# Probabilities times V with V as the stationary operand, two heads side by side on two column groups

## The reference, cut to what matters

```
branch A: logits over the top-k admissible keys, probs = softmax(logits)
          attn_a = probs @ v
branch B: window of 128 plus the own chunk, one learned sink per head in the denominator
          attn_b = (p @ v) / denom
o_a = (attn_a * silu(z_a)) @ w_oa        o_b = (attn_b * silu(z_b)) @ w_ob
y   = x + gate * ((sigmoid(g_a) * o_a + sigmoid(g_b) * o_b) @ w_out)
```

## Time and profile before

| what | us |
|---|---|
| median of 3 runs (1081.9 to 1086.25) | 1082.78 |
| the profiled execution, its own time | 1083.33 |
| its span | 1081.5 |
| PE busy / weight loads busy | 1035.2 / 920.8 |
| DVE / ACT / POOL busy | 676.3 / 408.9 / 323.3 |
| L1613, matmuls by V, forms with `VA`: 576 instructions, busy | 74.9 |

### The profile page before, as it was taken

How to read it: one execution, slowest core, us unless ns; L and a number is a source line. 1 busy time by engine, 2 the same in 40 slices (tenths; PEclk the granted TensorE clock), 3 DMA queues, 4 the chain that set the end, 5 groups by cost and what they waited for, 6 DMA issues and landing times.

```text
span 1081.5 us, 18078 instructions
## 1 busy us (share of the span) xinstructions
PE 1035.2 (96%) x6569; PEld 920.8 (85%) x6569; DVE 676.3 (63%) x1437; ACT 408.9 (38%) x1239; POOL 323.3 (30%) x348
## 2 busy tenths in 40 slices
PE   6976999999999999999999999999999999999998
PEld 1336888787799999999998998888888689999998
DVE  2647337699999999999951676555464454331111
ACT  0245456544432322222113676665564452212000
POOL 0034003221243532122124434332130034536432
PEclk9988999999999999999999799999999979999999
DMA  9822001473332323232134732112100646524332
GB/s 348 329 74 64 23 32 64 121 243 101 98 95 81 108 79 116 78 90 88 48 134 152 253 100 72 35 60 74 35 23 20 191 150 196 163 82 132 122 121 75
DMA packets 100586, 120.83 MB, mean 112 GB/s; under 512 B 11128, under 2 KB 83592, under 8 KB 99352
## 3 DMA queue, kind: packets, MB, share of 16 engines
q1 hardware_dynamic: 95344, 114.48, 33.5%
q10 hardware_dynamic: 5160, 5.24, 1.4%
HBM read 89.72 MB, written 35.95 MB: 116 GB/s over the span
## 4 chain that ended last, share of the span: by engine, by line
PE 85%; issue 4%; DVE 3%; ACT 3%; DMA 2%; POOL 2%; SPq 0%; POOLq 0%; DVEq 0%
PE PS L1360 18%; PE PS L1362 18%; PE PS L1361 18%; PE PS L1613 9%; PE PS L1589 6%; PE PS L1534 4%; PE PS L1369 4%; PE PS L1553 2%; PE PS L1592 2%; PE PS L1435 2%; POOL YO L872 1%; DVE HL L1155 1%; DVE XT L1173 1%; PE PS L1539 1%; DMA WADA<-in_w_ada 1%
## 5 line engine op out<-in xcount | busy, mean ns | idle before, releaser
L1362 PE MATMUL PS<-HH,WL 128*128 128x384 f32 (+1 forms) x576 | 187.9, 326 | 0.0
L1360 PE MATMUL PS<-HH,WH 128*128 128x384 f32 (+1 forms) x576 | 187.8, 326 | 0.0
L1361 PE MATMUL PS<-HL,WH 128*128 128x384 f32 (+1 forms) x576 | 187.7, 326 | 0.0
L1214 DVE MAX8 M<-SC 128x8 f32<-128x384 f32 (+3 forms) x210 | 174.8, 870 | 10.5 <-DVE SC L1219 10.0
L1219 DVE MATCH_REPLACE8 SC<-M,SC 128x384 f32<-128x384 f32 (+3 forms) x210 | 180.0, 864 | 0.0
L767 POOL TENSOR_TENSOR WL<-RAW,WH 128x512 fp32r<-128x512 f32 (+1 forms) x80 | 100.6, 1263 | 246.4 <-ACT WH L888 246.4
L1360 PE MATMUL PS<-WH,HH 128*128 128x512 f32 (+3 forms) x288 | 110.3, 383 | 8.1 <-DVE HL L1155 7.9
L1361 PE MATMUL PS<-WL,HH 128*128 128x512 f32 (+3 forms) x288 | 108.7, 377 | 0.0
L1362 PE MATMUL PS<-WH,HL 128*128 128x512 f32 (+3 forms) x288 | 108.5, 377 | 0.0
L1360 PEld LDWEIGHTS PS<-HH,WH 128*128 128x128 f32 x576 | 108.1, 188 | 0.1
L1361 PEld LDWEIGHTS PS<-HL,WH 128*128 128x128 f32 x576 | 108.1, 188 | 0.0
(11 more groups left out here) (180 smaller groups left out, 2066.1 us busy)
## 6 DMA issues: line engine op xcount, KB each, us to landing
RAW<-in_w_all SPq DMA_DIRECT2D x72, 256.0 KB, 2.7
WADA<-in_w_ada SPq DMA_DIRECT2D x8, 1536.0 KB, 20.3
gz<-STG SPq DMA_DIRECT2D x48, 192.0 KB, 1.8
snat<-STG SPq DMA_DIRECT2D x24, 256.0 KB, 2.0
QKV<-snat SPq DMA_DIRECT2D x8, 768.0 KB, 6.0
GT<-gz SPq DMA_DIRECT2D x32, 192.0 KB, 2.5
XN<-in_x_prompt SPq DMA_DIRECT2D x8, 512.0 KB, 16.9
btad<-bvd ACTq DMA_DIRECT2D x4, 1024.0 KB
```

The lines of the kernel that those rows point to most:

```text
L1214: V.max(M8[0:r, a, :], w).then_inc(sel_step, 1)
L1360: T.matmul(out, wh, mh, start=first, stop=False)
L1361: T.matmul(out, wh, ml, start=False, stop=False)
L1362: return T.matmul(out, wl, mh, start=False, stop=last)
```

## The change

1. PE takes the units in pairs. Heads are reordered to 0, 4, 1, 5, 2, 6, 3, 7, so that a pair has one head of each key/value head. In even steps s PE multiplies units s - 4 and s - 3; for every block of keys and both heads in turn, V (128 keys x 64) is the stationary operand and `PT` (128 keys x 128 queries) the moving one. The output is transposed already, 64 x 128, and goes to partitions 0 to 63 for the first head and 64 to 127 for the second.
2. The "A" transposes, `ATTN` and the multiplication into it are gone. The reciprocals are taken in step 8g + 9, written to device memory in transposed order (`rdd`), and read back broadcast over 64 partitions per key/value head (`RB`, two transfers, step 8g + 10). SP loads z straight to `ATS`, POOL multiplies it by `RB` in step 8g + 15, DVE multiplies bank 6 + branch by that in step 8g + 16, SP writes it out in step 8g + 17. For the last group the three are at 8g + 11, 12 and 13.
3. `PT` has three buffers in place of two. `PT2`, `XNB`, `XG`, `LG1` and `RB` lie at other addresses, `RDEN` has two buffers, the slots of `GT` are used in another order, and the columns of z and the rows of `w_oa` and `w_ob` are permuted on the host to match the order of the pairs.

```
         VBS = at("VBS", [128, 2, 128], F32, 132608)
-        XNB = at("XNB", [128, 20, HD], F32, XB + 6144)
-        XG = at("XG", [128, 20, HD], F32, XB + 12288)
-        LG = [at("LG0", [128, 1024], F32, XB), at("LG1", [128, 1024], F32, XB + 17408)]
-        ATTN = [at("ATTN0", [128, 512], F32, XB + 4096), at("ATTN1", [128, 512], F32, 67584)]
+        XNB = at("XNB", [128, 20, HD], F32, XB + 8192)
+        XG = at("XG", [128, 20, HD], F32, XB + 13312)
+        LG = [at("LG0", [128, 1024], F32, XB), at("LG1", [128, 1024], F32, XB + 4096)]
...
-        ZT = at("ZT", [128, 4, 128], F32, XB + 21504)
-        PT = at("PT", [128, 2, 1024], F32, SCB + 8192)
+        RB = at("RB", [128, 4, 128], F32, 67584)
+        PT = [at("PT0", [128, 1024], F32, SCB + 8192), at("PT1", [128, 1024], F32, SCB + 12288),
+              at("PT2", [128, 1024], F32, XB + 18432)]
...
 
-        UNITS = [(tt, br, h) for tt in range(NT) for br in range(2) for h in range(8)]
+        HEADS = [4 * (i % 2) + i // 2 for i in range(8)]
+        UNITS = [(tt, br, h) for tt in range(NT) for br in range(2) for h in HEADS]
         NU = len(UNITS)
...
             TP[16 * (2 + i) + 6].append(("C", i, 0))
-        for g in range(2 * NT):
-            TP[8 * g + 15].append(("A", g // 2, g % 2))
         TQ = [(s, x) for s in range(S0, S1) for x in TP[s]]
...
         LOAD_AT, NORM_AT, SPLIT_AT = -7, -5, 2
+        NG2 = 2 * NT
+        ZR_AT = {8 * g + (15 if g < NG2 - 1 else 11): g for g in range(NG2)}
+        FIN_AT = {8 * g + (16 if g < NG2 - 1 else 12): g for g in range(NG2)}
+        OUT_AT = {8 * g + (17 if g < NG2 - 1 else 13): g for g in range(NG2)}
 
...
         for q, (_, x) in enumerate(TQ):
-            if x[0] == "A":
-                EV.append("V")
-            elif x[0] == "P" and unit_keys(x[1]) > 512:
+            if x[0] == "P" and unit_keys(x[1]) > 512:
                 EV.append("SV"[x[2]])
...
                 full, part = min(4, nk // 128), nk % 128 if nk < 512 else 0
-                dst = PT[:, u % 2, 512 * j:512 * (j + 1)].rearrange("p (b n) -> p b n", b=4)
-                if u >= 2:
-                    eng.wait_ge(pv_pe, u - 1)
+                dst = PT[u % 3][:, 512 * j:512 * (j + 1)].rearrange("p (b n) -> p b n", b=4)
+                if u >= 3:
+                    eng.wait_ge(pv_pe, (u - 3) // 2 + 1)
                 if full:
...
                 last = copy(QT[x[1] % 2][:, 4 * x[2]:4 * x[2] + 4, 0:r], src[:, :, 0:r])
-            elif x[0] == "A":
-                g, r = 2 * x[1] + x[2], rows_of(x[1])
-                if g >= 2:
-                    eng.wait_ge(att_out[g % 2], 16 * (g // 2))
-                eng.wait_ge(zt_in, 16 * (g + 1))
-                last = nc.vector.tensor_tensor(ATS[:, g % 2, :, 0:r], src[:, :, 0:r], ZT[:, :, 0:r], ALU.mult)
             else:
...
                     sp.dma_start(QKV[0:rows_of(tt), tt % 2, :], snat[tcols(tt), :]).then_inc(qkv_in[tt % 2], 16)
-                if s % 8 == 0 and 8 <= s < NU + 8:
+                if s % 8 == 1 and 9 <= s < NU + 8:
                     g = s // 8 - 1
+                    r = rows_of(g // 2)
+                    if g >= 2:
+                        sp.wait_ge(att_out[g % 2], 16 * (g // 2))
+                    sp.dma_start(ATS[:, g % 2, :, 0:r],
+                                 gz[512 * (g % 2):512 * (g % 2) + 512, tcols(g // 2)].rearrange("(b p) n -> p b n", p=128)).then_inc(zt_in, 16)
+                    sp.wait_ge(rden_done, g + 1)
+                    sp.dma_start(rdd[g, :, 0:r].rearrange("h q -> q h"), RDEN[0:r, g % 2, :], allow_slow_non_contiguous=True).then_inc(rdd_out, 16)
+                if s % 8 == 2 and 10 <= s < NU + 8:
+                    g = s // 8 - 1
+                    r = rows_of(g // 2)
+                    sp.wait_ge(rdd_out, 16 * (g + 1))
                     if g >= 1:
-                        wait_evac(sp, TIDX[("A", (g - 1) // 2, (g - 1) % 2)])
-                    sp.dma_start(ZT[:, :, 0:rows_of(g // 2)],
-                                 gz[512 * (g % 2):512 * (g % 2) + 512, tcols(g // 2)].rearrange("(b p) n -> p b n", p=128)).then_inc(zt_in, 16)
+                        sp.wait_ge(zr_done, g)
+                    for kv in range(2):
+                        sp.dma_start(RB[HD * kv:HD * (kv + 1), :, 0:r],
+                                     bass.AP(rdd.tensor, 1024 * g + 512 * kv, [[0, HD], [128, 4], [1, r]])).then_inc(rb_in, 16)
                 tt = prep(s, SPLIT_AT)
...
                         sp.dma_start(t["pb_k"], XNB[0:r, 18:20, :]).then_inc(k_out, 16)
-                for x in TP.get(s - 1, []):
-                    if x[0] == "A":
-                        tt, br = x[1], x[2]
-                        g = 2 * tt + br
-                        wait_evac(sp, TIDX[x])
-                        sp.dma_start(attd[512 * br:512 * (br + 1), tcols(tt)].rearrange("(b p) n -> p b n", p=128),
-                                     ATS[:, g % 2, :, 0:rows_of(tt)]).then_inc(att_out[g % 2], 16)
+                if s in OUT_AT:
+                    g = OUT_AT[s]
+                    tt, br = g // 2, g % 2
+                    sp.wait_ge(att_done, g + 1)
+                    sp.dma_start(attd[512 * br:512 * (br + 1), tcols(tt)].rearrange("(b p) n -> p b n", p=128),
+                                 ATS[:, g % 2, :, 0:rows_of(tt)]).then_inc(att_out[g % 2], 16)
 
...
                     last.then_inc(qs_lo, 1)
+                if s in ZR_AT:
+                    g = ZR_AT[s]
+                    r = rows_of(g // 2)
+                    pool.wait_ge(zt_in, 16 * (g + 1))
+                    pool.wait_ge(rb_in, 32 * (g + 1))
+                    z = ATS[:, g % 2, :, 0:r]
+                    nc.gpsimd.tensor_tensor(z, z, RB[:, :, 0:r], ALU.mult).then_inc(zr_done, 1)
...
             act.wait_ge(min_done, NU)
-            act.wait_ge(pv_pe, NU)
+            act.wait_ge(pv_pe, NU // 2)
...
                         t_evac(dve, V.tensor_copy, x, tev_dve)
-                if (s - 11) % 8 == 0 and 11 <= s <= NU + 3:
-                    g = (s - 11) // 8
+                if s % 8 == 1 and 9 <= s <= NU + 1:
+                    g = s // 8 - 1
                     tt, br = g // 2, g % 2
...
                         link(V.tensor_tensor(DEN[0:r, 1, :], DEN[0:r, 1, :], ES[0:r, 0, :], ALU.add))
-                    link(V.reciprocal(RDEN[0:r, :], DEN[0:r, br, :]))
-                    dve.wait_ge(pv_pe, 8 * (g + 1))
                     if g >= 2:
-                        dve.wait_ge(tr_pe, TIDX[("A", (g - 2) // 2, br)] + 1)
-                    V.tensor_tensor(ATTN[br][0:r, :].rearrange("p (h d) -> p h d", h=8),
-                                    bank(6 + br)[0:r, :].rearrange("p (h d) -> p h d", h=8),
-                                    RDEN[0:r, :].unsqueeze(2).broadcast_to([r, 8, HD]), ALU.mult).then_inc(att_done, 1)
+                        dve.wait_ge(rdd_out, 16 * (g - 1))
+                    V.reciprocal(RDEN[0:r, br, :], DEN[0:r, br, :]).then_inc(rden_done, 1)
+                if s in FIN_AT:
+                    g = FIN_AT[s]
+                    r = rows_of(g // 2)
+                    dve.wait_ge(pv_pe, 4 * (g + 1))
+                    dve.wait_ge(zr_done, g + 1)
+                    z = ATS[:, g % 2, :, 0:r]
+                    V.tensor_tensor(z, bank(6 + g % 2).rearrange("p (b n) -> p b n", b=4)[:, :, 0:r], z, ALU.mult).then_inc(att_done, 1)
 
...
                         last = T.transpose(out[0:m, 128 * (b % 4):128 * (b % 4) + r], PB[u % 3][0:r, 128 * b:128 * b + m], IDF[0:r, 0:r])
-                elif x[0] == "A":
-                    g, r = 2 * x[1] + x[2], rows_of(x[1])
-                    pe.wait_ge(att_done, g + 1)
-                    for b in range(4):
-                        last = T.transpose(out[:, 128 * b:128 * b + r], ATTN[x[2]][0:r, 128 * b:128 * (b + 1)], IDF[0:r, 0:r])
                 else:
...
                         transposes(x)
-                if 0 <= s - 3 < NU:
-                    u = s - 3
+                if 0 <= s - 3 < NU and s % 2 == 0:
+                    u = s - 4
                     tt, br, h = UNITS[u]
                     r, nk = rows_of(tt), unit_keys(u)
-                    wait_evacs(pe, last_t(u))
+                    wait_evacs(pe, last_t(u + 1))
                     g = 2 * tt + br
...
                     kb = (nk + 127) // 128
-                    kv = slice(HD * (h // 4), HD * (h // 4) + HD)
                     for b in range(kb):
                         m = min(128, nk - 128 * b)
-                        if br == 0:
-                            v = VAS[0:m, b, kv] if tt == SAMPLE else VA[0:m, b, kv] if tt else VA0[:, kv]
-                        else:
-                            v = VBS[0:m, b, kv] if tt == SAMPLE else VB[0:m, max(tt - 1, 0) + b, kv]
-                        last = T.matmul(bank(6 + br)[0:r, HD * h:HD * (h + 1)], PT[0:m, u % 2, 128 * b:128 * b + r], v,
-                                        start=(b == 0), stop=(b == kb - 1))
```

(26 more changed lines are left out.)

4 lines of the change are left out of this document (2 added, 2 removed).

## The result

The changed kernel takes 1164.84 us (median of 4 runs, 1162.26 to 1170.76) against 1082.93 us before, a ratio of 1.075 with a 95% interval of 1.0728 to 1.0772: **82 us slower**. 1058 had been forecast, within 1044 to 1092. Some executions of a kernel take 1 to 1.5% longer than its others at a lower mean clock (the kernel before once 1099 us at 0.954, against 1084 at 0.972), so medians are compared.

A forecast was written before the change was run, and what follows sets the result against it. PE, busy 96% of the span, was taken as the bound. From 1083.3 us, -35.9 + 14.1 - 2.6 - 9.9 + 4 + 5.8 = -24.5 us gave 1058.8, about 1058 us for the median; range 1044 to 1092.

The forecast's parts named there:

- e, the way of the reciprocals: Write, broadcast and POOL's product from step 8g + 9: about 9.1 us, hidden with 1 us to spare, cost 0.
- The third rival: Broadcast lands late, DVE stands 5 us in step 8g + 16 of 8 groups, PE behind it: 1098 us, chance 0.07.
- QKV moved ahead: SP no longer holds the QKV load behind the attention transposes, so its 6.2 us are covered before POOL's product.
- a, the swap: Product by V in prompt tiles: 816 instructions at 62 ns instead of 106, column groups side by side, -35.9 us.
- The first two rivals: Product by V: one stream at a time, 108 ns, 1094 us, chance 0.22; half a gain, 81 ns, 1074 us, chance 0.16.
- b, the changes of shape: Each switch of PE's array shape costs 0.11 us: +14.1 us in prompt pairs, -2.6 us in the sample.
- c: The attention transposes on PE go, with the idle time before them: -9.9 us.
- d: In odd steps PE has little work while the second head's transposes are copied; some 35 pairs lose 0.12 us: +4 us.
- f, the end: After the last exponential nothing covers the trip, and `WOL[0]` comes behind POOL's product: +5.8 us.

The follow-up runs named there:

- e_contig: Changed kernel with the reciprocals written in 128 runs of 32 bytes, not 1024 single elements (output wrong, timing only): 1076.9 us, ratio 0.9927.
- e_write_only: Kernel before plus the transposed single-element write of the reciprocals once per group through SP's queue, its values never read: 1142.35 us, ratio 1.0545.
- e_apart: As e_bcast, but in each pair all blocks of the first head come before all of the second: 1096.72 us (one run).
- e_bcast: Changed kernel without the trip through device memory; PE transposes the spread reciprocals and DVE multiplies z by them: 1073.26 us, ratio 0.9894.
- e_full2: Changed kernel with reciprocals transposed on PE, written in 512-byte runs, table split, `WOL[0]` earlier, projection loads behind group 15's broadcast: 1065.18 us, ratio 0.9838.
- e_contig_wol: As e_contig, but POOL splits `WOL[0]` in step 146, before waiting for the last group's broadcast: 1073.31 us, ratio 0.9878.
- e_contig_bta: As e_contig, but the 3 MB bias table is loaded in three 1 MB parts, each behind a broadcast: 1067.67 us, ratio 0.9817.
- e_write_actq: As e_write_only, but the writes are issued by ACT through its own queue, in step 8g + 13: 1109.62 us, ratio 1.0233.

## Why the prediction was wrong, point by point

- **e, the way of the reciprocals: the step that failed.** It priced the write with the landing of the `attd` row, 3.5 us, and the sum of 9.1 us left 1 us of cover (1.8 by its own parts a to c: 13.5 - 1.4 + 0.9 - 0.6 = 12.4 us for a group of branch B, 10.9 for seven steps). That row is a transfer of 256 KB in runs of 512 bytes; the write is 4 KB in 1024 runs of 4 bytes. Bytes were compared where the runs decide. Measured are 10.6 us for the write and 16.1 us for the way. e_contig shows it: in 128 runs of 32 bytes the same 4 KB need 1.4 us, and the time falls by 88 us.
- **The third rival had the mechanism and less than half the size.** It named the place (DVE in step 8g + 16, PE behind it) and the threshold (landings above 4 us), and gave it 0.07. It counted 8 groups at 5 us, 40 us in all; 14 groups waited, and the time is 107 us above the forecast. It took what PE loses to be just DVE's wait in each group, and left out that each group is held by the one before through DVE's order, that the end pays the latency once more without cover, and that PE's gaps lower the clock. The evidence it set against itself, ZT's 3.1 us, was again a row of long runs.
- **The price had no row of its own.** The kernel before holds no transfer with such short runs in the attention. It was the one place where a bound from above was due, and 3.5 us was no bound. The Trainium skill, "DMA: Bandwidth & Descriptors" (Specifications), gives 512 B as the least transfer for full rate, with a read-modify-write below it; it has no figure for what 4-byte runs cost. The runs agree with it in so far as the 4-byte runs are dear, 10.6 us for 1024 of them. But 128 runs of 32 bytes, which are below 512 too, land in 1.4 us, hardly later than 8 runs of 512 bytes in 1.2, so that limit isn't what decides here.
- **QKV moved ahead: borne out.** SP issues it behind the broadcast, so it isn't held by the write; it lands after 5.3 us, and POOL's wait for it falls from 86.5 to 20.6 us. What the part left out is the other transfer behind the write: `attd` lands after 11.1 us instead of 3.5. That such a write also costs by what it delays is shown by e_write_only (54 to 57 us), not priced anywhere in the prediction.
- **a, the swap: right.** 62 ns were taken, 59 measured, so 816 x 47 ns = 38 us on PE instead of 35.9. Why it works is shown by e_apart. The first two rivals, together 0.38, are both refuted by the 59 ns: neither 108 nor 81. The ratio of the Trainium skill, "TensorE: Matmul & The Clock Gate" (Part 3), as the prediction applied it gave an estimate of 68 ns. The same part's rule that a load overlaps a running matmul only when their row groups differ is spoken against once more by 59 ns with two column groups on the same rows.
- **b, the changes of shape: right.** 0.09 and 0.11 us against 0.11.
- **c and d** can't be read from the changed kernel, whose PE waits anyway. e_bcast has the transposes back and lands at 1073; e_full2 without them, but with a small one per group, at 1065. How much the short odd steps cost wasn't isolated.
- **f, the end: right in kind, too small in size** by the same write: 12.2 us from the last exponential to the projection were forecast, 22.3 measured, 10.3 with the write in runs of 32 bytes. `WOL[0]` is what waits, as e_contig_wol shows.
- **Not foreseen:** the 3 MB table in SP's queue between the first write and its broadcast, 9 us (e_contig_bta). The kernel before issues it in the same step (L667), so it could have been seen. In the same way the last prompt group's broadcast stands behind the loads for the output projection. With the write repaired and these out of the way the kernel is at 1065 us, 7 us above the forecast; how these are shared among c, d and f stays open.

## What to carry to other kernels

Price a transfer by the length and number of its runs, not by its bytes, and from a row with the same runs; if there is none, the cost has no upper bound yet, and a chain of waits can multiply it by the number of groups. A matmul that is bound by loading its stationary operand gains from swapping the operands when two column groups alternate matmul by matmul (here two instructions each). Before moving a small result through device memory, transpose it where it is cheap (one PE transpose of 128 x 8 per group here), and look at what is issued behind it, on any queue.

## What the runs showed of the hardware

- A write of 4 KB to device memory in 1024 elements of 4 bytes takes 10.6 us to its landing, in 128 runs of 32 bytes 1.4 us. It isn't a price per run alone: the sample's writes of 512 such elements still take 9.0 and 9.1 us. The packets themselves have nearly all started within 2.2 us of the issue. What fixes the rest stays open. From 700 to 793 us the DMA share is 0.48 in the changed kernel and 0.58 in e_write_only, 0.22 in e_contig and 0.18 in the kernel before, but also only 0.23 in e_write_actq, whose writes go through ACT's queue.
- Transfers issued close behind it land later, on the same queue (QKV 13.1 us instead of 6.3, `attd` 11.1 instead of 3.5) and on another one (`attd` 9.7 instead of 3.5, e_write_actq). A queue of its own doesn't shield them; QKV, issued 7 to 10 us behind, lands after 8.4 us.
- Two fp32 streams of 128 columns on column groups 0 to 63 and 64 to 127 run side by side, with their loads hidden: 59 ns per instruction, 102 ns if each group's instructions come in one block.
